# Ten of sixteen stretches of attention probabilities turned in 32x32 blocks, the blocks carried by ScalarE and GpSimd

## The chip, the cores and the metric

The kernel runs on one core of one Trainium2 chip. The metric is the device time in microseconds (us) of one execution. Engines have short names in the profile: PE is TensorE, DVE is VectorE, ACT is ScalarE, POOL is GpSimd and SP is SyncE, which issues most loads.

## What is computed

Two sequences of 512 tokens with 1024 features ("trunks", b = 0 and 1 in the kernel) go through one layer each: neighbourhood attention with 16 heads of 64, then 16 experts of which each picks its 64 best tokens of a trunk's 512, and a last norm. All in float32:

```python
def trunk(x, ...):
    u = rmsnorm(h, norm_mix_g[i])
    mix = neighbourhood_attention(u, na_w_qkv[ia], na_rpb[ia], na_w_o[ia])
    h = h + mix
    u = rmsnorm(h, norm_ffn_g[i])
    h = h + expert_choice_ffn(u, router_w[i], moe_w_gate[i], moe_w_up[i], moe_w_down[i])
    return rmsnorm(h, final_norm_g)

# in neighbourhood_attention, for each row r of the 8x64 grid
    s = einsum('bchd,bicjhd->bhcij', q_r, k_win) + bias
    p = softmax(s.reshape(B, NA_HEADS, GRID_W, kh * NA_KW), axis=-1)
    out = einsum('bhcij,bicjhd->bchd', p, v_win)
```

## The kernel before

**Stages.** Attention of trunk 0 takes about the first 230 us, attention of trunk 1 the time to about 450 us, and the experts the rest. Every large product is made of three matmuls of rounded parts (high x high, high x rest, rest x high). So each 1 MB pair of weights is rounded on ACT (`high`, w_high) and subtracted on DVE (`rest`, w_rest) before PE uses it.

**Groups.** A trunk's 16 heads go in four groups of four (`first_group`, `second_group`, `third_group`, `last_group`; group numbers g = 0 to 3). Each group has two stretches of two heads (0 and 1, then 2 and 3). There are 16 stretches in both trunks. The order of each engine's work is written out by hand in the functions of these names, one set for each engine, and the engines meet at semaphores. Each engine does its list in order.

**One stretch.** PE makes the scores (`score`); DVE adds the biases and finds the maxima (`biased`); ACT takes the exponentials (`exponentials`); DVE normalises (`normalise_rows`). The probabilities then lie with queries on the partitions and have to be turned for the product with v (`values`). There are two ways:
- whole: PE turns them in 28 transposes (`turn_probabilities`, line 2199), and ACT and DVE copy them out of PSUM (`copy_pt`, lines 900 and 1486). 12 stretches.
- by blocks: DVE transposes all 32x32 blocks of a head in place of their rows (`turn_blocks_pt`, line 1492), and ACT carries the 16 blocks of partitions and windows to where they belong, both heads at once, in 16 copies of 32 partitions by 512 (`move_pt`, line 909). 4 stretches: heads 0 and 1 of groups 0 and 2.

**Around them.** PE fills the time between scores and values with projections: v for two groups at once (`project_v`), q and k of the next group (`project_t`, jobs q0, k0, q1, k1, 24 matmuls each) and the output projection (`project_out`, jobs w0 to w7). The next group's q and k are copied out of PSUM by DVE (`copy_q`, `copy_k`), rounded by ACT (`cast_qk`) and subtracted by DVE (`rest_qk`, two SBUF inputs), and `score` waits for that. `split_ot` on ACT and then DVE does the same for a stretch's output, which frees PSUM bank 4 and feeds `project_out`. `shift_v` on ACT issues two DMAs that make a copy of v shifted by 64 partitions (v_off, semaphore voff_in); the first `values` of a group wait for it. In trunk 0, ACT also squares parts of the next trunk's x (`next_piece`) and takes their root (`root(1)`, with a table of its own on ACT), and DVE makes the norm from it (`one_over_rms(1)`).

**POOL** in attention: a memset after the pieces, then for each trunk the loads or stores of x and h at the trunk's ends. It computes nothing between.

## Time and profile before

| | |
|---|---|
| median of 3 runs | 1520.5 us (1519.72 to 1521.24) |
| profiled execution | 1520.91 us, its span 1519.1 us |
| PE busy | 1505.3 us, 99% |
| DVE busy | 1316.2 us, 87% |
| ACT busy | 1250.3 us, 82% |
| POOL busy | 330.1 us, 22% |
| TensorE clock granted | 0.999 of full speed |

Times in the rows are of one profiled execution and count from the start of its span. An operation's length is its own; successive matmuls overlap, so the distance between starts is what a matmul costs PE. "idle before" is the time an engine stood still ahead of an operation, and the arrow names what ended that.

### The profile page before, as it was taken

What the parts mean: (1) busy time and instruction counts of PE and PEld (TensorE: products, weight loads), DVE (VectorE), ACT (ScalarE), POOL (GpSimd) and SP (SyncE); (2) the same over time, 40 slices, a digit from 0 to 9 for tenths busy, and PEclk for the clock granted to TensorE, in tenths of its full rate; (3) what the DMA queues carried; (4) which work ended last, traced back from release to release, by engine and by line L of the source; (5) the groups of instructions that cost most, each with busy time, mean ns of one, the idle gap of its engine ahead of it and who ended that gap; (6) DMA issues with size and microseconds to landing.
All of it is one profiled execution on the core that took longest, in us unless ns stands there. A gap on an engine that the chain in (4) does not pass through costs nothing.

```text
span 1519.1 us, 22067 instructions
## 1 busy us (share of the span) xinstructions
PE 1505.3 (99%) x7738; PEld 1217.5 (80%) x7738; DVE 1316.2 (87%) x1415; ACT 1250.3 (82%) x1491; POOL 330.1 (22%) x154
## 2 busy tenths in 40 slices
PE   9999999999999999999999999999999999999997
PEld 7888878888863888888888888888888888888886
DVE  7684786785865899999999999999999999999988
ACT  6756656546453799999999999999999999999997
POOL 0000001000022232242322523233242322420103
PEclk9999999999999999999999999999999999999999
DMA  9633447433476999999999999999999999999998
GB/s 346 193 137 124 154 140 265 124 125 111 151 248 225 395 420 391 415 400 404 407 406 405 397 411 391 398 407 399 412 388 404 405 393 414 395 414 382 387 396 349
DMA packets 156407, 498.59 MB, mean 328 GB/s; under 512 B 10880, under 2 KB 36608, under 8 KB 156352
## 3 DMA queue, kind: packets, MB, share of 16 engines
q1 hardware_dynamic: 144624, 461.54, 77.6%
q0 software_dynamic: 9280, 31.07, 6.6%
q10 hardware_dynamic: 2448, 5.25, 1.3%
q8 instruction: 34, 0.56, 0.1%
q14 instruction: 21, 0.17, 0.0%
HBM read 473.70 MB, written 20.97 MB: 326 GB/s over the span
## 4 chain that ended last, share of the span: by engine, by line
PE 89%; ACT 3%; DVE 3%; DMA 2%; issue 2%; SPq 0%; POOLq 0%; POOL 0%; ACTq 0%; DVEq 0%
PE ps L2093 76%; PE ps L2142 4%; PE ps L2149 2%; ACT w_high L1253 2%; PE ps L2258 2%; DVE w_rest L1404 2%; PE ps L2193 1%; PE ps L2414 1%; DMA raw<-w_gate 1%; PE ps L2199 1%; DMA u_rows<-arena 1%; ACT arena L1224 1%; DMA raw<-w_qkv 1%; PE ps L2696 0%; PE ps L2410 0%
## 5 line engine op out<-in xcount | busy, mean ns | idle before, releaser
L1404 DVE TENSOR_TENSOR w_rest<-raw,w_high 128x2048 fp32r<-128x2048 f32 x212 | 477.9, 2283 | 40.9 <-ACT w_high L1253 25.1
L1253 ACT CAST w_high<-raw 128x2048 fp32r<-128x2048 f32 x184 | 352.1, 1915 | 17.6 <-PE ps L2093 14.7
L2093 PE MATMUL ps<-w_high,xt_high 128*128 128x512 f32 x984 | 305.2, 390 | 0.7 <-DVE w_rest L1404 0.6
L2093 PE MATMUL ps<-w_rest,xt_high 128*128 128x512 f32 x984 | 304.3, 389 | 0.0
L2093 PE MATMUL ps<-w_high,xt_rest 128*128 128x512 f32 x984 | 304.2, 389 | 0.0
L2093 PEld LDWEIGHTS ps<-w_high,xt_high 128*128 128x128 f32 x984 | 184.1, 188 | 41.5 <-DVE w_rest L1404 2.4
L1404 DVE TENSOR_TENSOR w_rest<-early,w_high 128x2048 fp32r<-128x2048 f32 x90 | 204.4, 2286 | 13.3 <-ACT w_high L1253 13.3
L2093 PEld LDWEIGHTS ps<-w_high,xt_rest 128*128 128x128 f32 x984 | 184.7, 188 | 38.4
L2093 PEld LDWEIGHTS ps<-w_rest,xt_high 128*128 128x128 f32 x984 | 184.7, 188 | 38.3
L1404 DVE TENSOR_TENSOR w_rest<-raw_more,w_high 128x2048 fp32r<-128x2048 f32 x92 | 206.0, 2274 | 4.7 <-ACT w_high L1253 4.7
L1224 ACT COPY arena<-arena 32x256 f32<-32x256 f32 x464 | 187.3, 404 | 10.6
L1253 ACT CAST w_high<-early 128x2048 fp32r<-128x2048 f32 x90 | 172.2, 1915 | 10.9 <-PE ps L2093 8.9
L1253 ACT CAST w_high<-raw_more 128x2048 fp32r<-128x2048 f32 x92 | 175.8, 1912 | 2.9 <-PE ps L2093 1.9
L827 POOL DMA_INDIRECT h_rows<-xh,rows x15 | 109.5, 7302 | 303.4 <-ACT xh L1235 303.4
L784 POOL DMA_INDIRECT xh<-u_rows,aff x60 | 136.5, 2275 | 82.3 <-DVE v L1910 54.6
L2093 PE MATMUL ps<-ut_high,w_high 128*128 128x512 f32 x240 | 96.2, 401 | 0.3 <-DVE w_rest L1553 0.3
L2093 PE MATMUL ps<-ut_rest,w_high 128*128 128x512 f32 x240 | 93.7, 390 | 0.0
L2093 PE MATMUL ps<-ut_high,w_rest 128*128 128x512 f32 x240 | 93.6, 390 | 0.0
L895 ACT ACTIVATE arena<-arena,nmx 128x256 f32<-128x256 f32 x128 | 63.3, 496 | 33.4 <-DVE nmx L1482 33.4
L2093 PE MATMUL ps<-w_high,ht_high 128*128 128x512 f32 x256 | 78.9, 389 | 0.0
L2093 PE MATMUL ps<-w_high,ht_rest 128*128 128x512 f32 x256 | 78.8, 389 | 0.0
L2093 PE MATMUL ps<-w_rest,ht_high 128*128 128x512 f32 x256 | 78.8, 389 | 0.0
(319 smaller groups left out, 2304.0 us busy)
## 6 DMA issues: line engine op xcount, KB each, us to landing
raw<-w_down SPq DMA_DIRECT2D x64, 1024.0 KB, 8.8
raw<-w_gate SPq DMA_DIRECT2D x62, 1024.0 KB, 8.2
raw<-w_up SPq DMA_DIRECT2D x62, 1024.0 KB, 9.6
raw_more<-w_down SPq DMA_DIRECT2D x32, 1024.0 KB
early<-w_down SPq DMA_DIRECT2D x32, 1024.0 KB, 8.0
raw_more<-w_gate SPq DMA_DIRECT2D x31, 1024.0 KB
raw_more<-w_up SPq DMA_DIRECT2D x31, 1024.0 KB
early<-w_gate SPq DMA_DIRECT2D x31, 1024.0 KB, 9.5
```

Source lines behind the costliest of these rows:

```text
L784: pool.indirect_dma_start(xg[:, t * SPAN:(t + 1) * SPAN], None, u_pieces, at).then_inc(gathered, 16)
L827: pool.indirect_dma_start(h_dram, bass.IndirectOffsetOnAxis(ap=rows[:, e:e + 1], axis=0), ys, None, compute_op=ALU.add).then_inc(scattered ...
L895: nc.scalar.activation(scores[hh % 2][:, i, :], scores[hh % 2][:, i, :], ACT.Exp, bias=nmx[:, hh % 2, i:i + 1], accum_out=psum_row[:, hh % ...
L1224: nc.scalar.copy(to_chunks[columns, :, tokens], from_blocks[tokens, :, columns]).then_inc(turn_step[h], 1)
L1253: nc.scalar.copy(w_high[:, i % SLOTS, :], src).then_inc(high_done, 1)
L1404: nc.vector.tensor_tensor(w_rest[:, j, :], src, w_high[:, j, :].bitcast(F32), ALU.subtract).then_inc(rest_done, 1)
L2093: done = nc.tensor.matmul(out, lhs, rhs, start=start and part == 0, stop=stop and part == 2)
L2142: nc.tensor.matmul(out[i], tokens[:, at], w_high[:, j:j + SHARED, kc * GC:(kc + 1) * GC], start=kc == 0 and tokens is ut_high, stop=False)
L2149: last = nc.tensor.matmul(out[i], ut_high[:, at], w_rest[:, j:j + SHARED, kc * GC:(kc + 1) * GC], start=False, stop=kc == KC - 1)
L2193: last = nc.tensor.matmul(bank(PAIR_BANKS[half], 2)[:, at + begin:at + end], queries[on, tile * P:(tile + 1) * P], keys[on, lo + begin:lo ...
L2199: return nc.tensor.transpose(bank(PAIR_BANKS[half] + r)[:, at:at + HD], scores[half][on, i, c * P:(c + 1) * P], ident[on, on])
L2258: last = nc.tensor.matmul(out, vals, probabilities[:, each * lo:each * hi, n, :], start=c == first, stop=c != first)
```

## The change

`by_blocks` now names five of a trunk's eight stretches, ten in all: both of groups 0 and 2, and the second of group 1. PE's `turn_probabilities(A, 2)` and the copies behind it are gone from the first three groups. The 16 moves of a stretch are shared: ACT does the first 8 and POOL the last 8, each POOL copy waiting for the one before it. POOL's ten rounds of moves stand in its list ahead of the trunk's next loads. `values` waits for both. On DVE, `biased` of heads 2 and 3 comes ahead of the split of the first output, each head is transposed right behind its normalisation, and the subtractions of the pairs v2, v3, w2 and w3 (`rest_pair`) come later. In the first group PE makes job k0 (of the next group) behind the scores of heads 2 and 3 instead of ahead of the values of heads 0 and 1. In the third group ACT's casts of q and k stand ahead of the square and root of the next trunk, and Exp's table is loaded right behind the root, ahead of `split_ot`. Two semaphores of the experts' start are merged into one, with no other effect. The diff, cut to its core:

```diff
 def by_blocks(n):
-    return n % HEADS // GROUP % 2 == 0 and n % GROUP < PAIRED
+    return (n % HEADS // GROUP, n % GROUP // PAIRED) in BY_BLOCKS
+BY_BLOCKS = ((0, 0), (0, 1), (1, 1), (2, 0), (2, 1))
+        def block_of(n):
+            a, c = n % QUARTERS, n // QUARTERS
+            queries, keys = slice(a * QUARTER, (a + 1) * QUARTER), slice(c * QUARTER, (c + 1) * QUARTER)
+            return (arena[keys, 0:TILES:TILES - 1, a * WIN:(a + 1) * WIN], arena[queries, 1:TILES - 1, c * WIN:(c + 1) * WIN])
 # GpSimd
+            def move_pt(A):
+                pool.wait_ge(pt_dve, A + PAIRED)
+                before = MOVES // 2 * turned_by_blocks(A) // PAIRED
+                for n in range(MOVES // 2):
+                    if n:
+                        pool.wait_ge(pt_carried, before + n)
+                    nc.gpsimd.tensor_copy(*block_of(MOVES // 2 + n)).then_inc(pt_carried, 1)
+                pool.wait_ge(pt_carried, before + MOVES // 2)
+            def move_blocks(b):
+                for g, p in BY_BLOCKS:
+                    move_pt(head_count(b, g) + PAIRED * p)
             pool.wait_ge(eps_done, 1 + QUARTERS)
+            move_blocks(0)
             pool.wait_ge(piece_done, PIECES)
...
                     pool.dma_start(*rows_of(xh, x, b)).then_inc(xh_in, 16)
+                    move_blocks(b)
 # ScalarE
             def move_pt(A):
                 act.wait_ge(pt_dve, A + PAIRED)
-                for n in range(MOVES):
...
+                for n in range(MOVES // 2):
+                    nc.scalar.copy(*block_of(n)).then_inc(pt_moved, 1)
             def first_group(b):
...
+                cast_qk(b, 1, "q", 0)
                 split_ot(A, 0, 0)
-                cast_qk(b, 1, "q", 0)
-                cast_qk(b, 1, "k", 0)
                 exponentials(A, 2)
                 exponentials(A, 3)
+                cast_qk(b, 1, "k", 0)
+                move_pt(A + PAIRED)
                 if b == 0:
                     next_piece(1)
-                copy_pt(A, 2)
-                copy_pt(A, 3)
             def second_group(b):
...
-                copy_pt(A, 2)
-                copy_pt(A, 3)
+                move_pt(A + PAIRED)
             def third_group(b):
...
                 exponentials(A, 2)
                 exponentials(A, 3)
+                move_pt(A + PAIRED)
+                cast_qk(b, 3, "q", 0)
+                cast_qk(b, 3, "k", 0)
                 if b == 0:
                     next_piece(8)
                     root(1)
-                copy_pt(A, 2)
-                copy_pt(A, 3)
-                cast_qk(b, 3, "q", 0)
-                cast_qk(b, 3, "k", 0)
+                    nc.scalar.preload_act_table(ACT.Exp)
                 split_ot(A, 2, 1)
 # VectorE, first_group
                 copy_q(b, g, 0)
-                copy_k(b, g, 0)
-                split_ot(b, g, 0)
                 biased(A, b, g, 2)
                 biased(A, b, g, 3)
+                split_ot(b, g, 0)
                 normalise_rows(A, 2)
+                turn_blocks_pt(A, 2)
+                copy_k(b, g, 0)
                 normalise_rows(A, 3)
+                turn_blocks_pt(A, 3)
                 rest_qk(b, g + 1, "q", 0)
                 rest_qk(b, g + 1, "k", 0)
                 copy_q(b, g, 1)
-                copy_pt(A, 2)
-                copy_pt(A, 3)
 # VectorE, second_group
-                split_ot(b, g, 0)
                 biased(A, b, g, 2)
                 biased(A, b, g, 3)
+                split_ot(b, g, 0)
+                normalise_rows(A, 2)
+                turn_blocks_pt(A, 2)
+                normalise_rows(A, 3)
+                turn_blocks_pt(A, 3)
+                copy_q(b, g, 0)
                 rest_pair(b, "v", 2)
-                normalise_rows(A, 2)
-                normalise_rows(A, 3)
-                copy_q(b, g, 0)
-                rest_pair(b, "v", 3)
                 copy_k(b, g, 0)
-                copy_pt(A, 2)
-                copy_pt(A, 3)
                 rest_qk(b, g + 1, "q", 0)
                 rest_qk(b, g + 1, "k", 0)
                 copy_q(b, g, 1)
+                rest_pair(b, "v", 3)
                 split_ot(b, g, 1)
 # VectorE, third_group
-                split_ot(b, g, 0)
                 biased(A, b, g, 2)
                 biased(A, b, g, 3)
+                split_ot(b, g, 0)
+                normalise_rows(A, 2)
+                turn_blocks_pt(A, 2)
+                normalise_rows(A, 3)
+                turn_blocks_pt(A, 3)
+                copy_q(b, g, 0)
+                copy_k(b, g, 0)
                 rest_pair(b, "w", 2)
-                normalise_rows(A, 2)
-                normalise_rows(A, 3)
+                rest_qk(b, g + 1, "q", 0)
+                rest_qk(b, g + 1, "k", 0)
                 if b == 0:
                     mean_square(1)
-                copy_q(b, g, 0)
+                split_ot(b, g, 1)
                 rest_pair(b, "w", 3)
-                copy_k(b, g, 0)
-                copy_pt(A, 2)
-                copy_pt(A, 3)
-                rest_qk(b, g + 1, "q", 0)
-                rest_qk(b, g + 1, "k", 0)
-                split_ot(b, g, 1)
                 if b == 0:
                     one_over_rms(1, True)
 # TensorE
             def values(A, b, g, hh):
                 if by_blocks(A + hh):
-                    pe.wait_ge(pt_moved, MOVES * (turned_by_blocks(A) // PAIRED + 1))
+                    carried = MOVES // 2 * (turned_by_blocks(A + hh - half) // PAIRED + 1)
+                    pe.wait_ge(pt_moved, carried)
+                    pe.wait_ge(pt_carried, carried)
             def first_group(b):
                 project_t(b, g, "q0", q)
-                project_t(b, g, "k0", k)
                 values(A, b, g, 0)
                 values(A, b, g, 1)
                 score(A, b, g, 2)
                 score(A, b, g, 3)
+                project_t(b, g, "k0", k)
                 project_t(b, g, "q1", q)
-                project_t(b, g, "k1", k, 0, KC // 2)
-                turn_probabilities(A, 2)
-                project_t(b, g, "k1", k, KC // 2, KC - 1)
+                project_t(b, g, "k1", k, 0, KC - 1)
             def second_group(b):   # and third_group
-                turn_probabilities(A, 2)
```

## Rows read from the trace of the kernel before

**Rows 1.** The page, parts 1 and 2: busy us (share) and instructions; granted PE clock.
```profile
PE 1505.3 (99%) x7738; PEld 1217.5 (80%) x7738; DVE 1316.2 (87%) x1415; ACT 1250.3 (82%) x1491; POOL 330.1 (22%) x154
PEclk9999999999999999999999999999999999999999
```

**Rows 2.** Windows (stretch, its length, then busy us and instructions by engine); turns, grouped.
```profile
162.40:173.49 11.09, 11.09 (x50) 8.90 (x48) 10.89 (x34) 6.15 (x20) 0.21 (x1) 1.00 0.51 163
173.49:174.50 1.01, 1.01 (x29) 0.94 (x28) 0.90 (x2) 0.25 (x1) 0.00 (x0) 1.00 0.07 24
174.50:177.45 2.95, 2.95 (x16) 2.18 (x12) 2.33 (x4) 1.86 (x4) 0.00 (x0) 1.00 0.98 301
800.00:900.00 100.00, 100.00 (x443) 82.84 (x442) 97.26 (x51) 96.41 (x95) 29.71 (x12) 1.00 1.02 402
...
L2199 PE MATMUL ps<-ident,arena 64*128 64x64 f32 x336 | 13.1, 226 | 0.0
```

**Rows 3.** ACT's 16 moves; POOL's copies and multiplies, grouped: busy, mean ns | idle before.
```profile
138.00 10.24 ACT L909 COPY arena<-arena 32x512 f32<-32x512 f32 x16
...
L818 POOL TENSOR_TENSOR xh<-xh,grow 128x1024 f32<-128x1024 f32 x15 | 36.2, 2411 | 194.4 <-DVE w_rest L1404 192.1 <-DMA xh<-u_rows,aff 2.3
L837 POOL CAST xt_high<-v 128x1024 fp32r<-128x1024 f32 x14 | 14.6, 1045 | 128.2 <-DVE w_rest L1404 128.2
L792 POOL COPY v<-ident 32x128 f32<-32x128 f32 x4 | 1.2, 292 | 0.2
```

**Rows 4.** Timeline of DVE and ACT, third group, trunk 0: start, length, operation [idle before].
```profile
129.12 2.36 DVE L1492 STREAM_TRANSPOSE arena<-arena 128x1024 f32<-128x1024 f32 x2
...
163.99 0.51 ACT L895 ACTIVATE arena<-arena,nmx 128x256 f32<-128x256 f32 x1 [2.35 <-DVE nmx L1482]
...
171.18 2.28 DVE L1404 TENSOR_TENSOR w_rest<-raw,w_high 128x2048 fp32r<-128x2048 f32 x1
173.60 0.69 DVE L1506 TENSOR_TENSOR early<-ps,grow 128x512 f32<-128x512 f32 x1
175.87 1.29 DVE L1572 TENSOR_TENSOR qk<-early,qk 128x512 fp32r<-128x512 f32 x2 [0.33 <-ACT qk L916]
```

**Rows 5.** Timeline at the end of the kernel: a DVE square and a POOL multiply.
```profile
1499.45 1.22 DVE L2032 CUSTOM_DVE_ANT_0 xh<-arena 128x1024 f32<-128x1024 f32 x1
...
1499.97 2.96 POOL L858 TENSOR_TENSOR arena<-arena,grow 128x1024 f32<-128x1024 f32 x1 [17.83 <-ACT xh L873]
```

**Rows 6.** Timeline, first group, trunk 0 (last v job, shift of v, values); landing of the second shift.
```profile
53.99 0.39 PE L2093 MATMUL ps<-ut_high,w_high 128*128 128x512 f32 x1
...
64.96 0.55 PE L2258 MATMUL ps<-arena,v 128*64 128x128 f32 x8
...
54.98 1.26 ACT L921 ACTIVATE v<-ps,rstd 128x512 f32<-128x512 f32 x2
...
57.07 0.62 ACTq L929 DMA_DIRECT2D v_off<-v  x1
...
DMA to landing us min/median/max: 5.0/5.0/5.1
...
137.41 0.69 ACT L921 ACTIVATE v<-ps,rstd 128x512 f32<-128x512 f32 x1 [1.12 <-PE ps L2149]
```

**Rows 7.** Timeline around the last group's first turn, trunk 0 (ACT, DVE, PE), then trunk 1.
```profile
168.67 1.28 ACT L890 ACT_TABLE_LOAD   x1
...
181.50 0.42 DVE L1478 CUSTOM_DVE_ANT_0 arena<-ps,bias_sb 128x256 f32<-128x256 f32 x1
187.50 1.14 DVE L1501 TENSOR_SCALAR arena<-arena,rinv 128x256 f32<-128x256 f32 x4
...
189.08 1.08 PE L2199 MATMUL ps<-ident,arena 64*128 64x64 f32 x28
...
406.56 1.14 DVE L1501 TENSOR_SCALAR arena<-arena,rinv 128x256 f32<-128x256 f32 x4
...
409.17 0.27 PE L2199 MATMUL ps<-ident,arena 64*128 64x64 f32 x1
```

More of the change, by code:

```diff
@@ L426, in encoder_kernel @@
         third_in = [sem(f"third_in{m}") for m in range(2)]
-        third_early, third_used = sem("third_early"), sem("third_used")
+        third_mm = sem("third_mm")
+        pt_carried = sem("pt_carried")
         third_silu_done, third_hid_done = sem("third_silu_done"), sem("third_hid_done")
@@ L904, in move_pt @@
                 act.wait_ge(pt_dve, A + PAIRED)
-                for n in range(MOVES):
-                    a, c = n % QUARTERS, n // QUARTERS
-                    queries, keys = slice(a * QUARTER, (a + 1) * QUARTER), slice(c * QUARTER, (c + 1) * QUARTER)
-                    into, of = arena[keys, 0:TILES:TILES - 1, a * WIN:(a + 1) * WIN], arena[queries, 1:TILES - 1, c * WIN:(c + 1) * WIN]
-                    nc.scalar.copy(into, of).then_inc(pt_moved, 1)
+                for n in range(MOVES // 2):
+                    nc.scalar.copy(*block_of(n)).then_inc(pt_moved, 1)
             def cast_qk(b, g, what, m):
@@ L1245, in highs @@
                     elif i % SLOTS in THIRD_SLOTS:
-                        act.wait_ge(third_used, 1)
+                        act.wait_ge(third_mm, 2)
                     if split_first:
@@ L1270, in _ @@
             nc.scalar.copy(by_trunk(xt_high)[:, 0, :, :], by_chunk[0]).then_inc(xth_done, 1)
-            act.wait_ge(third_early, 1)
+            act.wait_ge(third_mm, 1)
             nc.scalar.activation(third_silu[0:CAP, :], bank(THIRD_BANKS[0])[CAP:P, :], ACT.Silu).then_inc(third_silu_done, 1)
             rows_high(0)
-            act.wait_ge(third_used, 1)
+            act.wait_ge(third_mm, 2)
             nc.scalar.activation(third_silu[CAP:P, :], bank(THIRD_BANKS[0])[0:CAP, :], ACT.Silu).then_inc(third_silu_done, 1)
@@ L1490, in turn_blocks_pt @@
                 dve.wait_ge(norm_done, TILES * (A + hh + 1))
-                probabilities = scores[hh].rearrange("p i (c b j) -> p b (i c) j", c=2, b=QUARTERS)
-                nc.vector.transpose(pt[hh], probabilities).then_inc(pt_dve, 1)
+                probabilities = scores[hh % 2].rearrange("p i (c b j) -> p b (i c) j", c=2, b=QUARTERS)
+                nc.vector.transpose(pt[hh % 2], probabilities).then_inc(pt_dve, 1)
             def normalise_rows(A, hh):
@@ L1953, in _ @@
             first_rest_of_rows(1)
-            dve.wait_ge(third_used, 1)
+            dve.wait_ge(third_mm, 2)
             dve.wait_ge(third_silu_done, 2)
@@ L2318, in third_group @@
                 project_t(b, g, "k0", k)
-                turn_probabilities(A, 2)
                 project_t(b, g, "q1", q, 0, KC // 2)
@@ L2631, in _ @@
             first_rows()
-            early_third(KC - 1, KC).then_inc(third_early, 1)
+            early_third(KC - 1, KC).then_inc(third_mm, 1)
             pe.wait_ge(first_xt_done, 1)
@@ L2637, in _ @@
                 _, last = whole_gate_up(late_xt, kc, 2, slice(0, CAP), slice(CAP, P), kc == 0, kc == KC - 1)
-            last.then_inc(third_used, 1)
+            last.then_inc(third_mm, 1)
             places()
```

## The prediction

> **What bounds the kernel now.** I read the page's first two parts first. TensorE (PE) is busy for 99% of the span with its clock granted in full, against 87% for VectorE (DVE), 82% for ScalarE (ACT) and 22% for GpSimd (POOL) [rows 1]. The windows then show how dense "busy" is: in the expert stage 443 matmuls start in 100 us, one each 0.226 us, with no hole [rows 2]. The attention stage, the first 450 us, has the same pace. So PE's own order of work is the bound from end to end. A microsecond taken out of PE's list comes off the time, and any new wait of PE is added to it. The expert stage starts from what attention hands it, so it only shifts. The change touches attention alone.
>
> **What it removes.** Six of the twelve probability turns on PE go (second stretch of groups 0, 1 and 2, in both trunks). All twelve are 336 transposes, 28 each [rows 2]. In the third group of trunk 0, 48 matmuls, a turn and 12 matmuls take 11.09 + 1.01 + 2.95 = 15.05 us. Without the turn there are 60 matmuls in one run: 60 x 0.227 + 0.2 for one break in the flow = 13.8 us. Each turn is worth 1.23 us with the break that it causes, six are worth **7.4 us**. The copies of turned probabilities out of PSUM go too (ACT and DVE), which hold nobody up.
>
> **What it adds.** A stretch turned in blocks needs two DVE transposes (1.2 us each) and then 16 copies of 32x512 that carry the blocks; before, ACT made all 16 in 10.24 us, 0.64 each [rows 3, 4]. Now ACT makes 8 (5.1 us) and POOL 8 beside them. Such a POOL copy isn't in the trace. From 32x128 at 0.292 and 128x1024 at 1.045 us [rows 3] a line gives 0.61 for 512 elements, and 0.04 for the wait of each on the one before makes 8 of them 5.2 us. The bounds of one are half of the 1.045 (0.52) and half of the two-input multiply at 2.41 (1.2) [rows 3]. I take 0.61, since those rows are the same one-input kind. By the Trainium skill (GPSIMD Engine Reference, § 3.1) 512 elements of a tight one-input loop take 769 ns; by that figure the sum below would be some 5 us higher.
>
> **Is the carrying done in time?** Let S be the end of the scores of heads 2 and 3. In the third group DVE now adds the biases from S - 0.6 (the split of the first output no longer stands ahead); exponentials follow 1.7 us behind and take 4.05 for both heads [rows 4]. On DVE the biases (8 of 0.42 overlapping, with what goes with them 3.3), the split 0.7, and twice a normalisation (1.14 and its reciprocal, 1.35) and a transpose (1.2) end, with their overlaps, at S + 8.1. PE wants the probabilities at S + 13.8. ACT is done at S + 13.3 and POOL, alone, at S + 13.4: it fits by 0.4 us. The second group has 72 matmuls to cover (S + 16.5) and its carrying starts at S + 8.4; the first has 69 (S + 15.9) and starts at S + 8.8.
>
> **But POOL is not alone.** The end of the trace shows a POOL multiply that started while a DVE operation with two SBUF inputs (a tile squared) still had 0.70 us to run: it took 2.96 us instead of 2.41, so 0.55 of those 0.70 were added [rows 5]. The 29 POOL operations of the expert stage wait for a w_rest subtraction to end [rows 3] and so run beside DVE work that reads PSUM. I take it that a POOL copy and such a DVE operation exclude each other. That is also what the Trainium skill states (SBUF — State Buffer, § Who interferes with whom: two SBUF inputs on VectorE against a GpSimd instruction that reads SBUF, a lock held for the whole instruction); the row agrees with it.
> In the third group POOL has carried 5 of its 8 when DVE wants the 2.28 us subtraction for w_o, right behind the copy of k at S + 11.2 + 0.7 [rows 4]. DVE waits for the copy under way (to S + 12.2) and then shuts POOL out to S + 14.5. Two copies and one of the two q/k subtractions (0.69 each [rows 4]) are left: S + 16.4, against PE at S + 13.8. That is **2.6 us** a trunk (1.5 where POOL gets 7 done first, 3.3 where both subtractions go first). In the second group a subtraction of that size stands at the head: one copy, 2.3 us shut out, 7 copies, one or two q/k subtractions give S + 17.3 against S + 16.5, **0.7 us** a trunk (0 to 1.3). In the first group only the q/k pair is in the way and 0.5 us is spare: nothing (0 to 0.9). In the first stretches of the first and third group PE comes 10 us after the carrying or more. Behind the moves ACT has the casts of the next q and k, and PE's next scores want DVE's subtraction of these: ready at S + 15.3 where PE comes at S + 15.5, so nothing of its own while ACT is in time. Sum for two trunks: **6.6 us** (3 to 10).
>
> **k0 moved behind the scores.** This widens the cover of the first group's second stretch and strips that of its first: PE reaches the values after 24 matmuls instead of 48, at 53.99 + 5.6 = 59.6 instead of 64.96 [rows 6]. Moves on ACT are done, but the shift of v is not. The last v job ends at 54.0; its copy follows 0.2 us behind PE and takes 0.69, the second shift DMA is issued 0.8 behind that (57.07 behind 56.25 before), at 55.7, and lands 5.0 us later [rows 6], at 60.7. PE waits **1.15 us**, in trunk 1 the same: 2.3 us (2 to 3.5, if 1 MB loads run beside it). This wait is new; before, 2.9 us were spare.
>
> **The third group's tail.** In trunk 0 the root of the next trunk's norm now stands behind the carrying, and Exp's table is loaded ahead of the split of the second output. From the end of the moves at 174.5 (all times of this paragraph have one turn less ahead): two casts 1.1, a square 0.7, table 1.28, root 0.2, table 1.28, split 0.6, then DVE's split 0.7, the w_o subtraction 2.2 that was moved here, and the norm 1.0: biases of the last group start at 183.6 instead of 181.5. The second head is normalised 7.1 us after that start, as before (181.50 to 188.64) [rows 7]: 190.7. PE gets to this turn at 186.6 (189.08 less two turns) and can use 0.5 us for its first half, so it would wait 3.6 us. With the carrying already 2.6 us late, part of that is common: PE comes at 189.2, the chain ends at 191.6 (it is held by the q/k subtractions), **1.8 us** are left, and 0.5 more before the scores of heads 2 and 3, which wait for the same DVE. In trunk 1 there is no root; the moved subtraction alone makes the biases 2.2 us later, against 1.5 us spare (407.70 to 409.17 [rows 7]) and the 0.5 of the turn's first half: **0.3 us**. Sum: 2.6 us (1 to 4.5).
> The later w_rest of v and w_o free their load slots up to 9 us later; those loads are used 25 us on, so nothing. SP's and POOL's DMAs keep their order; POOL's loads of x stand ahead of the moves or behind the last scores, where they waited anyway.
>
> **Sum.** -7.4 + 6.6 + 2.3 + 2.6 = +4.1 us on the profiled execution's 1520.9, 1525.0; the median of the runs shown is 0.4 lower, so **1524.6**. This case alone: 1521.5 to 1528.
>
> **Rivals.**
> 1. POOL's copies are not held up by DVE (the row at 1500 is one case of a multiply, not of a copy). Then the carrying fits, PE waits only for v (2.3) and, with nothing in common, 3.7 + 0.5 + 0.3 in the third group's tail: -7.4 + 6.8 = -0.6, 1520.0, no change. It decides at a POOL copy of 0.65 us; for it speaks that nothing in the trace is a copy beside such a subtraction.
> 2. The tail hides too (DVE's and ACT's chain 3 us shorter than I add it up, v lands sooner): the PE work taken out comes off nearly whole, faster by 4 to 6 us, 1514.5 to 1516.5. Against it: each of its parts has a row.
> 3. A POOL copy costs 0.8 us or more. At 0.8 with its wait the three groups wait 0.9, 1.6 and 3.9 us a trunk instead of 0, 0.7 and 2.6: +6 on the forecast, 1530; at 1.0 another 10. Against it: both one-input rows.
>
> **How the numbers follow.** Forecast 0.57, rival 1 0.15, rival 2 0.11, rival 3 0.17. The range 1516.5 to 1531 leaves out most of rival 2 and the upper part of rival 3. About 0.2% (3.0 us) can be told from no change: slower is two thirds of the forecast and rival 3 (0.56), within is the rest of the forecast and rival 1 (0.31), faster 0.13.
>
> **What would show it.** PE's list of waits would show seven new places in attention: for v_off by DMA before the first values of each trunk (1.1 us), for POOL at the second values of the second and third group (0.7 and 2.6 us in each trunk), and for DVE at the last group's turn of trunk 0 (1.8). POOL copies would be 0.6 us where DVE is free and 2.3 us longer where a w_rest runs. Six fewer turns take 168 transposes from 336. It is wrong if POOL's copies stay at 0.6 beside w_rest (rival 1), or if PE shows no wait for DVE at the last group of trunk 0 (rival 2).

## The result, and the profile after

The changed kernel takes **1529.9 us** (median; 1528.7 to 1531.2) against 1520.1 for the kernel before on the same chip: 1.0063 times as long, 95% interval 1.0049 to 1.0077, so 9.8 us slower. The forecast was 1524.6, slower, with a range up to 1531.0. The sign holds, and so do the mechanisms behind it, but the size is 2.4 times what was forecast, and a term as large as the whole surplus (the clock, 6.0 us) is one that the forecast didn't have.

| | before | after |
|---|---|---|
| median of the runs, us | 1520.1 | 1529.9 |
| profiled execution, its span | 1520.9, 1519.1 | 1530.0, 1528.0 |
| PE instructions, busy us | 7738, 1505.3 | 7570, 1504.8 |
| mean granted clock of PE | 0.999 | 0.994 |

The page of the changed kernel, part 1 (beside [rows 1]), and the groups of POOL's new copies (beside [rows 3]; busy us, mean ns | idle before), then the turns that are left on PE (beside [rows 2]; duration in ns min/median/max, first and last start).

```profile
PE 1504.8 (98%) x7570; PEld 1218.1 (80%) x7570; DVE 1330.5 (87%) x1415; ACT 1255.2 (82%) x1495; POOL 403.2 (26%) x234
...
L742 POOL COPY arena<-arena 32x512 f32<-32x512 f32 x80 | 72.9, 912 | 253.1 <-DVE arena L1511 248.8
...
L2218 PE MATMUL ps<-ident,arena x168: 221/222/274, 95.1 to 433.7; 64*128 64x64 f32 x168
```

168 transposes are gone, 7.4 us of work, and yet PE is busy as long as before. So PE did the rest more slowly: that is the clock. POOL's copies take 0.91 us in the mean, not 0.61. What PE waited for from 15 to 470 us, the attention stage, in the changed kernel and then in the kernel before (us in all, times, longest):

```profile
PE ps L2279 <- issue: 5.8, 3, 2.8
PE ps L2279 <- DMA v_off<-v: 4.0, 2, 2.7
PE ps L2112 <- DVE xh L1543: 0.7, 2, 0.4
...
PE ps L2212 <- DVE qk L1591: 0.4, 2, 0.3
PE ps L2218 <- DVE arena L1520: 0.4, 1, 0.4
```
```profile
PE ps L2452 <- ACT gv L990: 0.5, 1, 0.5
PE ps L2093 <- DVE xh L1524: 0.3, 1, 0.3
```

L2279 is the values. Nearly ten microseconds of waits are new: 4.0 for the shifted v, and 5.8 put down to "issue", which means that the profile shows no releaser. The next view names it. The windows over three of the places, each with the stretch behind it (columns as in [rows 2]; the number behind POOL's is PE's granted clock):

```profile
53.40:61.70 8.30, 5.61 (x25) 4.33 (x24) 3.92 (x2) 4.41 (x3) 0.61 (x1) 1.00 1.04 319
61.70:66.55 4.85, 4.83 (x57) 4.63 (x57) 1.71 (x6) 1.20 (x2) 0.00 (x0) 0.65 0.58 199
163.90:180.70 16.80, 13.98 (x64) 11.25 (x63) 14.08 (x37) 12.12 (x30) 7.73 (x9) 1.00 0.24 71
180.70:185.50 4.80, 4.80 (x57) 4.58 (x57) 1.65 (x2) 2.00 (x3) 0.14 (x1) 0.64 0.39 138
...
404.20:410.20 6.00, 6.00 (x57) 5.71 (x57) 2.13 (x2) 0.59 (x1) 0.00 (x0) 0.50 0.31 122
```

The row left out is the wait of trunk 1, 16.80 us with 13.99 of work. Each wait (8.30 us with 5.61 of work; 16.80 with 13.98) is followed by values and scores at a granted clock of 0.65, 0.64 and 0.50: part or all of the stretch at 1.2 instead of 2.4 GHz. The same 56 matmuls take 3.2 us at the full clock (1.69 for the values and 1.52 for the scores, in the kernel before). Here they take 4.8, 4.8 and 6.0.

Why PE waited at 177.9 us is in the timelines of POOL and DVE for that stretch (start, length, operation, idle before), and in the durations of POOL's eight copies there (min/median/max, ns):

```profile
173.82 6.74 POOL L742 COPY arena<-arena 32x512 f32<-32x512 f32 x6
...
175.17 0.69 DVE L1525 TENSOR_TENSOR early<-ps,grow 128x512 f32<-128x512 f32 x1 [2.24 <-PE ps L2112]
175.78 2.28 DVE L1423 TENSOR_TENSOR w_rest<-raw,w_high 128x2048 fp32r<-128x2048 f32 x1
178.18 1.90 DVE L1591 TENSOR_TENSOR qk<-early,qk 128x512 fp32r<-128x512 f32 x2
...
L742 POOL COPY arena<-arena x8: 608/610/2697, 172.5 to 179.6; 32x512 f32<-32x512 f32 x8
```

One copy lasts 2.70 us, and it is the one that meets DVE's 2.28 us subtraction. The two q/k subtractions, 0.69 us each alone [rows 4 have 1.29 for both], take 1.90 us beside the last copies. ACT had made its eight by 177.5 (172.38 and 5.12 us); POOL ended at 180.56 (173.82 and 6.74), and PE went on at 180.66. So POOL is the releaser that the view of waits didn't name.

The sum of the path, from the starts of PE's matmuls in the two traces:

| part | forecast | measured |
|---|---|---|
| six turns | -7.4 | -7.4 |
| carrying late, third group | +5.2 | +5.8 |
| carrying late, second group | +1.4 | +0.4 |
| wait for the shifted v | +2.3 | +4.1 |
| tail of the third group | +2.6 | +1.0 |
| clock at half behind three waits | none | +6.0 |
| sum | +4.1 | +9.9 |

The measured sum is that of attention up to 457 us. The changed kernel's execution came to its first projection 0.6 us sooner (17.6 against 18.2 us), ahead of what the change touches, and 0.3 us went behind attention, so the two profiled executions differ by 9.05 us. The medians differ by 9.8.

### The profile page after: what moved, and what is told of

Its sections match the earlier page's. It is cut to its first block, busy times and chain, and to the rows that moved or that the text cites. A ratio compares the mean times of both kernels' runs of the same rounds, so it can differ in the third digit from the quotient of the medians.

```text
span 1528.0 us, 21830 instructions
## 1 busy us (share of the span) xinstructions
PE 1504.8 (98%) x7570; PEld 1218.1 (80%) x7570; DVE 1330.5 (87%) x1415; ACT 1255.2 (82%) x1495; POOL 403.2 (26%) x234
## 4 chain that ended last, share of the span: by engine, by line
PE 88%; ACT 4%; DVE 3%; issue 3%; DMA 1%; SPq 0%; ACTq 0%; POOLq 0%; DVEq 0%
PE ps L2112 75%; PE ps L2161 4%; ACT w_high L1272 2%; PE ps L2168 2%; PE ps L2279 2%; PE ps L2431 2%; PE ps L2212 1%; DVE w_rest L1423 1%; ACT arena L1243 1%; DMA v_off<-v 1%; DVE arena L1497 1%; DMA raw<-w_qkv 0%; PE ps L2713 0%; PE ps L2427 0%; PE ps L2449 0%
## 5 line engine op out<-in xcount | busy, mean ns | idle before, releaser
L742 POOL COPY arena<-arena 32x512 f32<-32x512 f32 x80 | 72.9, 912 | 253.1 <-DVE arena L1511 248.8
L842 POOL TENSOR_TENSOR xh<-xh,grow 128x1024 f32<-128x1024 f32 x15 | 36.1, 2409 | 194.3 <-DVE w_rest L1423 192.1
```

Source lines behind the costliest of these rows:

```text
L742: nc.gpsimd.tensor_copy(*block_of(MOVES // 2 + n)).then_inc(pt_carried, 1)
L842: nc.gpsimd.tensor_tensor(tokens, tokens, weights, ALU.mult).then_inc(rows_scaled, 1)
```

## The experiments

Theory: two new kinds of wait of PE (for the shifted v, and for POOL's copies that DVE shuts out), and a clock that falls behind the long ones. The rivals were that something else slows the copies, that the clock has another cause, and that one part of the change alone explains the rest. "Before" is 1520.2 to 1520.6 us on the chips used.

**1. w2_late: nothing but the place of one subtraction.**

```diff
                 copy_k(b, g, 0)
-                rest_pair(b, "w", 2)
                 rest_qk(b, g + 1, "q", 0)
                 rest_qk(b, g + 1, "k", 0)
                 if b == 0:
                     mean_square(1)
+                rest_pair(b, "w", 2)
```

> The changed kernel with one line moved: in the third group VectorE's subtraction for the 2nd pair of w_o (2.28 us) goes behind the two q/k subtractions instead of ahead of them. Theory (a GpSimd copy and a VectorE operation with two SBUF inputs exclude each other, and TensorE's clock falls after the long idle): all eight GpSimd copies of the third group's second stretch take 0.61 to 1.0 us, none 2.6; the 60 matmuls there take 13.8 to 14.0 us instead of 16.75 in both trunks, and the half clock at 181 and 403 us is gone. That would be 2 x 2.9 + 1.6 + 2.8 = 10.2 us, but in trunk 0 the last group's first turn waits for ScalarE's root and table and for VectorE (its biases start at 187.7, some 1 us earlier at best), so TensorE, 4.5 us earlier, waits there for 3.5 us more: 1.0 left in trunk 0 and 5.7 in trunk 1, 6.7 us in all, 1523.2. Rival A (the copies are slow for another reason, such as each copy's wait on the one before, or ScalarE beside it): the copy of 2.7 us stays and so does the time, 1529.9. Rival B (the clock falls whatever TensorE waits): only the idles go, 1524.1 at most, with the half clock still at 400 us.

Measured: 1527.2 us (1524.1 to 1528.5), ratio to before 1.0042 (1.0028 to 1.0056). Its profiled execution, 1524.1, is the fastest of the five; no trace shows what the other four add. POOL's copies, then the windows over the third group's 60 matmuls, the 36 behind it, and the last group's turn and what follows:

```profile
L742 POOL COPY arena<-arena x8: 607/610/612, 170.6 to 175.3; 32x512 f32<-32x512 f32 x8
```
```profile
162.00:176.00 14.00, 13.96 (x64) 11.24 (x62) 9.51 (x32) 9.38 (x25) 4.88 (x8) 1.00 0.19 58
179.20:190.00 10.80, 8.52 (x40) 6.74 (x38) 9.54 (x34) 5.24 (x17) 0.00 (x0) 1.00 0.68 219
190.00:192.90 2.90, 1.94 (x29) 1.64 (x29) 2.44 (x8) 2.70 (x4) 0.00 (x0) 0.50 0.47 186
```

All eight copies take 0.61 us and the stall is gone: rival A falls. The half clock behind it is gone in both trunks, so rival B falls too. But 1523.2 was expected, and most of the gain was lost at the next place. PE, 4.5 us sooner by this group alone, stood still for 2.3 us ahead of the last group's first turn and 1.0 in its middle, and now the clock fell there (0.50); in trunk 1 it waited 1.3 us at the same place, which the expectation had as free. A wait that is taken away moves on to whatever was hidden behind it: by the lists, DVE's two subtractions of 2.28 us and ACT's root and table, which stand ahead of the last group's biases. Run 6 tests that.

**2. busy_waits: the waits filled with repeated work.**

```diff
+                if b == 0:
+                    project_t(b, g, "q0", q, 0, KC // 2, KC // 2)
                 project_t(b, g, "q0", q)
 ...
+                project_t(b, g, "q1", q, 0, KC // 2, KC // 2)
                 project_t(b, g, "q1", q, 0, KC // 2)
```
The third number closes the sum of the first pass; the second pass starts it anew, so the result is the same.

> The changed kernel with 12 more matmuls ahead of each long wait: the first half of q0 is done twice in the first group of trunk 0, the first half of q1 twice in the third group of both trunks. 12 matmuls take 2.75 us, as long as the idle that they fill, so nothing arrives later. Theory (the clock fell because TensorE stood still): no stretch of half clock, the values and scores behind the three waits take 1.69 and 1.52 us again: 1.6 + 1.6 + 2.8 us less. In trunk 0 the last group's first turn waits for VectorE, which hides half of the second: 1.6 + 0.8 + 2.8 = 5.2 us, 1524.7. Rival (the clock falls for another reason, such as the place or the load on the chip): the three stretches of half clock stay, 1529.9.

Measured: 1526.4 us, and all five runs between 1526.2 and 1526.9. The same three places:

```profile
61.90:65.20 3.30, 3.25 (x57) 3.11 (x57) 1.66 (x6) 1.21 (x2) 0.00 (x0) 1.00 0.88 299
179.30:182.50 3.20, 3.18 (x56) 3.08 (x56) 0.76 (x2) 2.06 (x3) 0.20 (x1) 1.00 0.61 215
402.00:405.25 3.25, 3.21 (x56) 3.08 (x56) 0.79 (x2) 0.59 (x1) 0.00 (x0) 1.00 0.61 248
```

PE arrives no earlier, does 36 matmuls more, and the kernel is 3.5 us faster than the changed one, because the clock stays up. So the clock fell because PE stood still. The saving is 3.5 and not 5.2. Part of the third group's share in trunk 1 is given back, too: PE, sooner by 2.8 us, now loses 0.9 us to DVE's chain at the last group's turn and scores, which was expected for trunk 0 alone.

**3. k0_alone: one part of the change on the kernel before.**

```diff
-                project_t(b, g, "k0", k)
                 values(A, b, g, 0)
                 values(A, b, g, 1)
                 score(A, b, g, 2)
                 score(A, b, g, 3)
+                project_t(b, g, "k0", k)
```
(ACT's cast and DVE's copy of k0 move as in the change, and with them DVE's biases of heads 2 and 3, ahead of the split.)

> The kernel before with one part of the change alone: k0 of the second head group behind the scores of heads 2 and 3 in the first group, with ScalarE's cast and VectorE's copy of it moved as in the change; all six turns stay on TensorE. Theory: the values of heads 0 and 1 wait 2.7 us in trunk 0 and 1.3 in trunk 1 for the shifted v, and the clock falls once, behind the first: 2.7 + 1.3 + 1.6 = 5.6 us slower than before, 1525.7. Rival A (the wait of 2.7 comes of the other parts, say of the transfers' new times): 1.15 twice, no half clock, 1522.4. Rival B (the waits are there, the clock's fall has to do with the third group's too): 1524.1.

Measured: 1526.4 us. PE's waits show the shifted v twice, 2.7 us in trunk 0 and 1.8 in trunk 1 (ACT makes all sixteen moves here and comes to v later):

```profile
PE ps L2258 <- DMA v_off<-v: 4.5, 2, 2.7
```

So k0's place, with these moves, makes the kernel some 6 us slower, and rival A falls. The clock stays at 1.00 behind that wait in the profiled execution (the values and scores behind it, columns as above):

```profile
61.90:65.10 3.20, 3.20 (x56) 3.04 (x56) 3.01 (x6) 0.68 (x2) 0.00 (x0) 1.00 0.73 232
```

That execution is one of two at 1524.6 us with a mean clock of 0.998; the other three took 1526.4 to 1526.8 at 0.997. In the profiled execution of run 9 (piece_late), 1526.7 us with an idle of 2.6 us there, the values and scores behind it run at 0.64. So the same idle is followed by the fall in some executions and not in others, and where it comes it costs about 2 us.

**4. first_back: the change without its first group** (its second stretch turned on PE again, k0 ahead of the values):

```diff
-BY_BLOCKS = ((0, 0), (0, 1), (1, 1), (2, 0), (2, 1))
+BY_BLOCKS = ((0, 0), (1, 1), (2, 0), (2, 1))
```

> The changed kernel with its first group as before: the second stretch of group 0 turned on TensorE again and k0 ahead of the values. Theory: two turns come back (2 x 1.23 = 2.5 us), the waits for the shifted v (2.7 and 1.3) and one fall of the clock (1.6) go: 3.1 us less, 1526.8. Rival (what the first group won by its covered carrying is worth more than the v wait, because the time reappears at the next wait): within 1 us of the changed kernel, 1529 to 1531.

Measured: 1526.3 us, within 0.5 of the theory: 3.6 us less than the changed kernel. The wait for v is gone, the three entries of 5.8 us at the values are still there: 2.8 us in the third group of each trunk and 0.2 in the second.

**5. one_input: what about DVE's subtraction shuts POOL out?**

```diff
-                rest_pair(b, "w", 2)
+                one_input(b, "w", 2)
 ...
+                nc.vector.tensor_scalar(w_rest[:, j, :], raw[:, j, :], 1e-4, None, ALU.mult).then_inc(rest_done, 1)
```

> The changed kernel with VectorE's subtraction for the 2nd pair of w_o in the third group (two inputs in SBUF, 2.28 us) replaced at the same place by a multiplication with a constant over the same tile (one input in SBUF, about as long or half as long). It leaves out that part of the split of w_o. Theory (what shuts GpSimd out is the second SBUF input of the VectorE operation): the GpSimd copies beside it keep to 0.61 to 0.7 us, the eight take 5.0 to 5.5 us, and the 60 matmuls take 13.9 us instead of 16.75. Rival (GpSimd is shut out by any long VectorE operation on SBUF): a copy there takes 2.5 us or, if the multiplication runs in half the time, about 1.5, and TensorE still waits 1.5 us or more.

The multiplication, then POOL's eight copies:

```profile
173.88 1.22 DVE L1603 TENSOR_SCALAR w_rest<-raw 128x2048 fp32r<-128x2048 f32 x1
```
```profile
L742 POOL COPY arena<-arena x8: 607/610/1636, 170.6 to 176.3; 32x512 f32<-32x512 f32 x8
```

The copy beside it takes 1.64 us: 1.03 more than alone, most of DVE's 1.22. The last copy takes 1.16, beside a q/k subtraction. PE still waits 1.6 us at the values, and the kernel takes 1527.0 us: the rival. The theory as it was put (the second SBUF input) is too narrow. A one-input operation that gets through 2048 elements in 1.22 us, where two inputs take 2.28, shuts POOL out as well. What does not, by the changed kernel's own trace: the copies of q and k, with one input in PSUM, and an operation that replaces values, 256 elements in SBUF in 0.40 us (POOL's copies beside them take 0.61 us). The Trainium skill says (SBUF — State Buffer, § Who interferes with whom) that the shared port goes to a VectorE operation in a two-port fast mode, or to one with two SBUF inputs against a GpSimd read. The trace agrees on both halves, as far as the pace of 1.22 us tells the mode; the forecast quoted only the second.

**6. third_mended: every cause in the third group taken away, the rest as in the change.**

```diff
                 add_out(b, g, "w", 4, 6)
+                half_rest_pair(b, "w", 2, 0, rest_half)
                 add_out(b, g, "w", 6, 8)
+                half_rest_pair(b, "w", 2, 1, rest_done)
 ...
                 rest_qk(b, g + 1, "k", 0)
+                rest_pair(b, "w", 3)
                 split_ot(b, g, 1)
 ... on ScalarE:
-                    root(1)
-                    nc.scalar.preload_act_table(ACT.Exp)
                 split_ot(A, 2, 1)
+                if b == 0:
+                    root(1)
+                    nc.scalar.preload_act_table(ACT.Exp)
```

The norm (`one_over_rms`) goes from the end of the third group to the last group, behind the copies of its second turn; ACT's rounding for w2 goes ahead of two pieces of x.

> The changed kernel with its third group mended throughout: the 2nd w_o subtraction in two halves, one between the additions of the w jobs and one behind them, the 3rd one behind the two q/k subtractions and ahead of the second split, ScalarE's root of the next trunk's norm and Exp's table behind its split of the second output, and the norm that reads the root just ahead of the diagonals that use it. The first group stays as in the change. Theory (the third group's idle is the two GpSimd copies held up; the wait that w2_late found behind it, 2.7 + 1.2 us in trunk 0 and 1.5 us in trunk 1 at the last group's first turn, is VectorE's two subtractions of 2.28 and the root ahead of the biases): 60 matmuls in 13.9 to 14.0 us, biases of the last group start right behind their scores (181 instead of 184.7 us), the turn waits 0.5 us at most, no half clock behind it. From the changed kernel 2.8 + 1.6 + 1.0 in trunk 0 and 2.8 + 2.8 in trunk 1 = 11.0 us less, some 0.5 given back: 1519.4. Rival (the last group's start is held by something else, such as the exponentials on ScalarE behind the casts): the turn waits 2 us or more again, 1523 or more.

Measured: 1520.5 us over eleven runs, 1.0002 (0.9993 to 1.0011), 9.5 us less than the changed kernel where 10.5 were expected. Ahead of the last group's turn nothing is waited for (1.01 us, as [rows 2]), so what w2_late ran into was this tail. Left are the shifted v (3.4 us in all) and 1.4 us at one addition, since the norm now stands ahead of the diagonals. The window behind the wait for v in trunk 0, and the one over the third group's 60 matmuls:

```profile
62.50:65.70 3.20, 3.20 (x34) 3.08 (x34) 1.68 (x2) 0.62 (x1) 0.00 (x0) 0.50 0.96 312
164.60:178.50 13.90, 13.90 (x62) 11.16 (x60) 9.47 (x32) 9.31 (x25) 4.88 (x8) 1.00 0.46 134
```

**7. mended_first_back: third_mended with the first group as before the change.**

> third_mended with its first group as before the change (second stretch turned on TensorE, k0 ahead of the values): the carrying in blocks stays for the second stretches of groups 1 and 2 alone. Theory: no wait for the shifted v and no clock's fall is left; four turns fewer than before at 1.23 us, 4.9, of which some 0.7 us is given back (0.15 a trunk in the third group, 0.3 at the last turn): 1516.3 against 1520.5 before. Rival (time taken out of TensorE's list here comes back at the next wait, as in w2_late): 1519 to 1521.

Measured: **1517.0 us** (1516.3 to 1517.5, eleven runs), 0.9978 (0.9969 to 0.9987). With four turns fewer and no wait for the shifted v the kernel is faster than before, by 3.2 us where 4.2 were expected. The norm ahead of the diagonals, which makes PE wait 1.4 instead of 0.4 us at one addition, is as large as the difference.

**8. mended_k0_split: third_mended with k0 parted after 3 of 8 steps.** DVE's copies of k0 and q1 stand behind both transposes.

> third_mended with k0 of the second head group parted: its first 3 of 8 steps (9 matmuls, 2.05 us) ahead of the values of heads 0 and 1, the rest behind the scores of heads 2 and 3, and VectorE's copy of k behind both transposes. Theory: the wait for the shifted v falls from 2.7 to 0.7 us in trunk 0 and from 1.3 to 0 in trunk 1, the clock doesn't fall, and the cover of the second stretch (69 less 9 matmuls, 13.8 us) still holds GpSimd's carrying, which now ends at 13.5 behind the start: six turns at 1.23 fewer, 7.4, less 0.7 + 0.7 and up to 0.5 in the first group: 1515.0 against 1520.5 before. Rival (the cover is too short once k0 is parted): a wait of 1 us or more for GpSimd in both trunks, 1517 or more.

Measured: 1519.3 us, 0.9996 (0.9987 to 1.0005): the rival's time. Its waits:

```profile
PE ps L2115 <- DVE xh L1544: 1.8, 2, 1.4
PE ps L2282 <- ACT arena L930: 1.7, 2, 0.9
PE ps L2282 <- DMA v_off<-v: 0.9, 1, 0.9
PE ps L2115 <- DVE early L1587: 0.8, 1, 0.8
```

Nine matmuls are too few for the shifted v in trunk 0 (0.9 us left) and too many for the moves (0.8 and 0.9 us in the two trunks). The rival named POOL for that wait; here both carriers end at 80.3 us, ACT with its cast of k (0.62 us) ahead of its moves, POOL with two copies beside the q/k subtractions (1.06 and 0.96 us). The last row is a wait for DVE's copy of the last k. As DVE and ACT stand here, k0 can't cover both.

**9 and 10. piece_late and load_late: why v is later in trunk 0.** Both are k0_alone with one transfer moved: ACT's 256 KB load behind the shift, and SyncE's 1 MB load ahead of it.

```diff
 # piece_late, ScalarE
-                if b == 0:
-                    next_piece(0)
                 cast_qk(b, 1, "q", 0)
                 split_ot(A, 0, 0)
+                if b == 0:
+                    next_piece(0)
 # load_late, SyncE
                 load_bias(b, 1, 0)
+                if b == 0:
+                    sp.wait_ge(voff_in, 32)
                 load_nth(n + 1)
```

> k0_alone (the kernel before with k0 moved) and one thing more: ScalarE's load of the first 256 KB piece of x, which in trunk 0 is issued right behind the two transfers that shift v and on the same queue, goes behind the split of the first output. Question: why the wait for the shifted v is 2.75 us in trunk 0 and less in trunk 1. Theory (half of the surplus is this load, whose packets run among v_off's: 1.05 MB in 4.5 us instead of 0.79 MB in 3.6): v_off is complete 0.9 to 1.0 us sooner, TensorE waits 1.8 us instead of 2.75 in trunk 0. Rival (only the late start of the packets counts, at 57.1 us, when 2.9 MB of other loads end): the wait stays at 2.6 to 2.8.

> k0_alone with one load held back: in trunk 0 SyncE's 1 MB load of the third v pair, which runs from 51 us, waits until v_off has landed. Theory (the packets of v_off start late because 2.9 MB of loads are ahead of them on the same 16 engines): the loads end at some 54.5 instead of 56.9 us, v_off's packets start behind their issue, at some 55.5 instead of 57.3, and TensorE's wait in trunk 0 falls by 1.4 to 1.8 us, to 1.0 to 1.4. Rival (ScalarE's queue starts them 1.4 us late for its own reasons): start at 57.3, wait 2.75 as before.

Measured: 1525.2 and 1526.1 us, and the wait in trunk 0 is 2.6 and 2.7 us: neither theory holds on this base. It was the wrong base: in k0_alone ACT makes sixteen moves, and in these three runs its shift is issued up to 57.0 to 57.3 us and the packets start right behind, whether loads run or not; v_off lands 4.6 us behind its issue. In the changed kernel the issue ends at 55.7, the loads run on to 57.6, and the packets start at 57.1, so there the loads can matter. Run 12 (best_six) holds the load back with the changed kernel's ACT list: its loads end at 55.2, the issue ends at 56.1 and the packets start at once. The transfers from 53 to 63 us in run 12, then those of the changed kernel in the same stretch, then in trunk 1 (median us from issue to landing last):

```profile
raw<-w_qkv SPq DMA_DIRECT2D x2, 1024.0 KB, 7.1
v_off<-v ACTq DMA_DIRECT2D x2, 384.0 KB, 4.5
```
```profile
raw<-w_qkv SPq DMA_DIRECT2D x1, 1024.0 KB, 4.9
v_off<-v ACTq DMA_DIRECT2D x2, 384.0 KB, 6.0
piece<-x ACTq DMA_DIRECT2D x1, 256.0 KB, 6.2
...
v_off<-v ACTq DMA_DIRECT2D x2, 384.0 KB, 4.4
```

6.0 us beside loads, 4.4 in trunk 1 without them, 4.5 in trunk 0 once the loads are out of the way. That run moved the piece, too, but piece_late shows that the piece alone is worth 0.15 us. third_mended lies between: the issue ends at 57.1, the loads at 58.2, the packets start at 57.7 and land in 5.5. What is not settled is how the late start comes about between the queues.

**11 and 12. best_four and best_six.** best_four is mended_first_back with the norm between the last group's two normalisations and one of the second group's two v subtractions behind the q/k subtractions, the other in the third group. best_six has that and all six turns in blocks:

```diff
                 project_t(b, g, "q0", q)
+                project_t(b, g, "k0", k, 0, 2)
                 values(A, b, g, 0)
 ...
                 score(A, b, g, 3)
+                project_t(b, g, "k0", k, 2, KC)
 ... with load_late, piece_late, and the cast and subtractions of the next q and k behind the moves
```

> mended_first_back (1517.0) with two more mendings: the norm that reads the root goes between the two normalisations of the last group's first stretch, where VectorE was idle for 0.6 us, instead of ahead of the diagonals, where it made TensorE wait 1.8 instead of 0.7 us; and of the two v subtractions in the second group one goes behind the q/k subtractions and one into the third group, so that none runs beside GpSimd's carrying. Theory: 1.0 + 2 x 0.25 less, 1515.5. Rival (VectorE has no room there, the half-turns or the third group start late): no gain, 1516.5 to 1518.

> All six turns in blocks with every cause taken away: best_four's third, second and last group; in the first group k0 parted behind its first 2 of 8 steps (6 matmuls, 1.4 us), the 1 MB load held until v_off has landed, the piece of x behind the first split, the q/k subtractions and ScalarE's cast of k behind the moves. Theory: v_off has landed when TensorE comes (0 to 0.3 us), GpSimd ends 14.1 us behind the scores against a cover of 14.5: six turns less, 7.4, and 0.5 given back: 1513.4. Rival (the cover of the first group's second stretch or the exponentials are still short by 0.5 to 1 us a trunk): 1514.5 to 1516.

Measured: **1516.4 us** (1515.6 to 1516.9), 0.9974 (0.9963 to 0.9984), and **1516.3 us** (1514.3 to 1516.3), 0.9971 (0.9958 to 0.9983). Both beat the kernel before by some 4 us and the changed one by 13.5. Windows over the second and the third group's stretch of best_four, then over the stretch ahead of the first values and the one of 63 matmuls behind their scores in best_six: PE is busy throughout, at the full clock. Under them stands the largest wait in attention that best_six has left.

```profile
99.50:116.00 16.50, 16.50 (x74) 13.39 (x72) 10.83 (x34) 12.74 (x32) 4.88 (x8) 1.00 0.40 137
160.80:174.80 14.00, 13.94 (x64) 11.24 (x63) 9.48 (x32) 9.41 (x25) 4.88 (x8) 1.00 0.41 132
```
```profile
53.80:60.70 6.90, 6.90 (x33) 5.46 (x31) 2.54 (x2) 4.41 (x3) 0.61 (x1) 1.00 0.64 181
63.90:78.40 14.50, 14.50 (x65) 11.75 (x63) 10.32 (x34) 10.38 (x28) 5.34 (x8) 1.00 0.68 244
...
PE ps L2117 <- DVE early L1589: 1.3, 2, 0.8
```

best_four was forecast at 1515.5 and gains 0.6 us on mended_first_back, not 1.5: in the profiled executions its attention is 1.0 us shorter, and about half of that is gone again in the expert stage. best_six was forecast at 1513.4 and misses by 3 us. Its last matmul starts 5.7 us sooner than before (1505.0 against 1510.8), so some 1.7 of the 7.4 went ahead of it: DVE's copy of the last k, behind the next group's biases, comes 0.4 us sooner than in best_four where PE comes 1.2 us sooner, and holds PE for 1.3 us in two trunks (the row above). The rest lies behind the last matmul, where that execution took 9.5 us and the one of the kernel before 8.3; of all fourteen profiled executions ten take 8.1 to 8.3 us there and four 8.9 to 9.5, and no run here says why. In the medians the two turns that best_six saves over best_four are not to be seen.

## Why the prediction was right in sign and short in size

**The removed turns.** 168 transposes gone, 1.23 us a turn: kept. best_four, with four turns fewer and no new wait, is 3.9 us faster than before where 4 x 1.23 = 4.9 were taken out.

**POOL's copy.** The line drawn through 32x128 and 128x1024 [rows 3] gave 0.61 us; the trace has 0.607 to 0.63 wherever DVE leaves POOL alone. Rival 3 (0.8 us or more) falls. The 769 ns that the Trainium skill states for 512 elements of a tight loop (GPSIMD Engine Reference, § 3.1) don't hold for this copy.

**Exclusion.** Read off one row, a multiply beside a square [rows 5], and it held for copies: 2.52 to 2.70 us beside a w_rest, 0.89 to 0.96 beside a q/k subtraction. It works both ways, as the forecast had it: w_rest takes 2.25 to 2.28 where it starts first and 2.38 to 2.70 where a copy is under way, the q/k subtraction up to 1.10. That two SBUF inputs are what it takes was too narrow (run 5); no term of the sum hangs on it, as every subtraction in the sum has two. For the third group 2.6 us a trunk was forecast and 2.9 measured; w2_late shows the cause. The second group was forecast at 0.7 a trunk and came to 0.3 in trunk 0 and 0.1 in trunk 1: POOL ended at 119.0 us, just as PE came. Rival 1 (no hold-up) falls.

**The shifted v.** 1.15 us in each trunk was forecast; 2.75 and 1.3 were measured. In trunk 1 the step is right. In trunk 0 the mis-sized term is the landing: 5.0 us from the issue of the second shift [rows 6] was taken for both. The four of the changed kernel (the longest is trunk 0's, and PE went on 6.6 us behind its issue):

```profile
DMA to landing us min/median/max: 5.0/5.0/6.5
```

The upper end of the range named for this term (3.5 us in all, "if 1 MB loads run beside it") had the cause but not the size. In the kernel before, the shift was issued 2 us later, up to 57.7 us, and the loads had ended at 57.3, so it landed in 5.0. Moving ACT's shift forward changed the surroundings of the transfer, not only its slack.

**The tail of the third group.** 2.6 us forecast, 1.0 measured (0.6 inside the turn, 0.35 ahead of the scores, in trunk 0; nothing in trunk 1). The chain was read rightly: w2_late and busy_waits met it at once, in trunk 0 and in trunk 1, when PE came sooner. The wait was short because PE itself came 1.9 us later than forecast, counted from the scores (1.6 of it the clock, 0.3 the third group's wait): a late PE hides a late DVE.

**The clock.** This is the step that wasn't there: a term put at nothing. PE's granted clock was taken as 1.00 throughout, because the page showed it so [rows 1], for a kernel in which PE never stood still for more than 0.5 us in attention. The forecast itself put waits of 1 to 3 us into it. Behind the three longest, 2.7 to 2.8 us each, the clock was at half, 6.0 us in this execution. With the clock kept up, busy_waits is 3.5 us faster; 1.8 of the rest came back as waits for DVE (0.8 and 0.9 at the last group's turns). Without it the sum is +3.9, beside the forecast +4.1; but that closeness is partly luck, v's 1.8 and the third group's 0.6 us too few against the tail's 1.6 and the second group's 1.0 too many.

**What would show it.** Of the seven announced waits the two for v and the two of the third group are there in size, that for DVE in trunk 0 at 0.6 and not at 1.8 us, and those of the second group are almost nothing (0.3 and 0.1). Rival 2 (all hidden) falls.

## What to carry to other kernels

When a change creates a wait on an engine that was never idle, price the wait and then what the clock does behind it: here a wait of 2.8 us cost up to 2.8 us more. When two engines share work in SBUF, list every operation of the other engine that falls into the stretch, by where its inputs lie and how fast it runs; moving one subtraction behind two others took a 2.9 us stall away. And after each wait that goes, look for the next chain that it hid, before calling the gain: of the 10 us that w2_late was to set free, some 7 came back, at the last group's turns (4.6 us of waits in the trace, and half clock behind them), until root, norm and subtractions were moved as well.

## What the runs showed of the hardware that was not expected

- **PE's clock falls to half behind an idle, but not behind every one.** Behind 2.2 to 2.8 us of standing still it was seen at 0.50 to 0.65 in the changed kernel (three times), first_back (twice), w2_late, third_mended and piece_late, and in one_input behind two shorter waits that follow each other (0.8 and 1.3 us). Behind 2.7 us for v in the profiled executions of k0_alone, load_late and w2_late it stayed at 1.00, as behind a single wait of 1.3 us. k0_alone's runs lie at 1524.6 and at 1526.4 to 1526.8, piece_late's at 1524.4 to 1524.5 and at 1525.9 to 1526.7; the one trace of each group shows no fall (k0_alone, 1524.6) and a fall (piece_late, 1526.7). So the fall seems to come in some executions of the same kernel, and to cost 1.5 to 2 us. busy_waits, without such an idle, has all its runs within 0.7 us. Which idles bring the fall, no run here settles.
- **A one-input VectorE operation on SBUF shuts GpSimd out, too**, where it runs at double pace: 1.03 of its 1.22 us (one_input).
- **The v shift landed in 6.0 us beside 2.9 MB of loads and in 4.4 to 4.5 without**, and most of the difference was its late start: 1.4 us between the end of its issue and its first packet.
